# 16x16 diagonal blocks of the triangular inverses by VectorE, two output slots of each RWKV half moved to between gram and inverse, and a cross-attention in which the heads follow one another

## The reference, cut to what matters

```
u = rmsnorm(h);  p = u @ w_in
o_dn = deltanet(p[:, :DN_COLS])      # 8 heads of 128, chunks of 128 tokens: 16 matrices
o_rw = rwkv7(p[:, DN_COLS:])         # 16 heads of 64, in two halves of 8 heads
h = h + concat(o_dn, o_rw) @ w_out
h = h + cross_attention(rmsnorm(h), rmsnorm(mem))    # 4 heads of 128, 256 memory rows
h = h + square(relu(rmsnorm(h) @ w1)) @ w2;  return rmsnorm(h)
```

```
a_strict = where(strict, (k * beta) @ k.T * decay, 0)
lower = a_strict + eye(128);   u, w = solve_triangular(lower, rhs)
```

## Time and profile before

| what | value |
|---|---|
| three runs of the kernel before | 3989.09, 3991.14, 3993.26 us (median 3991.14) |
| the profiled execution | 3994.92 us |
| its span, first to last instruction | 3991.7 us |
| mean granted TensorE clock | 0.955 of full speed |
| TensorE busy | 3712.8 us, 93% of the span |
| VectorE busy | 2413.6 us, 60% |
| ScalarE busy | 1502.7 us, 38% |
| GpSimd busy | 157.9 us, 4% |

### The profile page before, as it was taken

How to read it: one execution, slowest core, us unless ns; L and a number is a source line. 1 busy time by engine, 2 the same in 40 slices (tenths; PEclk the granted TensorE clock), 3 DMA queues, 4 the chain that set the end, 5 groups by cost and what they waited for, 6 DMA issues and landing times.

```text
span 3991.7 us, 54679 instructions
## 1 busy us (share of the span) xinstructions
PE 3712.8 (93%) x22418; PEld 3305.0 (83%) x22418; DVE 2413.6 (60%) x2621; ACT 1502.7 (38%) x1294; POOL 157.9 (4%) x159
## 2 busy tenths in 40 slices
PE   8996899999999999999999999777787969999998
PEld 8985699999988888888888989576676868888887
DVE  3544547977677766666666644456465445566656
ACT  3333333445434333433344433322222343343334
POOL 2000000000000000000000000122121000000000
PEclk8998899999999999999999999798787989999999
DMA  4451444556767765565554544000012425555554
GB/s 178 174 191 51 148 160 174 204 191 221 264 227 244 252 219 200 200 205 200 200 200 155 184 152 156 10 22 32 22 43 106 169 86 189 189 189 189 189 188 148
DMA packets 122889, 650.35 MB, mean 163 GB/s; under 512 B 10737, under 2 KB 43889, under 8 KB 49553
## 3 DMA queue, kind: packets, MB, share of 16 engines
q1 hardware_dynamic: 116224, 620.20, 44.5%
q0 software_dynamic: 6544, 28.44, 1.9%
HBM read 620.81 MB, written 27.79 MB: 162 GB/s over the span
## 4 chain that ended last, share of the span: by engine, by line
PE 87%; DVE 9%; ACT 2%; issue 1%; DMA 1%; DVEq 0%; ACTq 0%; POOL 0%; SPq 0%; PEldq 0%
PE pairs L2312 19%; PE pairs L2313 19%; PE pairs L2314 19%; PE quad L2357 12%; PE quad L2358 6%; DVE w_low L2057 2%; PE quad L2468 1%; PE pairs L2470 1%; PE quad L2398 1%; PE quad L2460 1%; PE quad L2865 1%; ACT w_high L1136 0%; PE quad L2703 0%; DVE arena L1940 0%; PE quad L2788 0%
## 5 line engine op out<-in xcount | busy, mean ns | idle before, releaser
L2057 DVE TENSOR_TENSOR w_low<-ring,w_high 128x2048 fp32r<-128x2048 f32 (+1 forms) x547 | 1253.2, 2292 | 926.8 <-ACT w_high L1136 926.3
L1136 ACT CAST w_high<-ring 128x2048 fp32r<-128x2048 f32 (+1 forms) x547 | 1039.2, 1901 | 1737.4 <-PE pairs L2314 1276.0
L2312 PE MATMUL pairs<-x_t,w_high 128*128 128x256 f32 x2592 | 745.4, 288 | 19.3 <-DVE w_low L2057 10.7
L2313 PE MATMUL pairs<-x_t,w_high 128*128 128x256 f32 x2592 | 738.8, 285 | 0.0
L2314 PE MATMUL pairs<-x_t,w_low 128*128 128x256 f32 x2592 | 738.8, 285 | 0.0
L2357 PE MATMUL quad<-x_t,w_high 128*128 128x512 f32 x1984 | 703.0, 399 | 9.9 <-DVE w_low L2057 9.9
L2312 PE MATMUL pairs<-w_high,act_high 128*128 128x512 f32 x1568 | 613.8, 391 | 10.2 <-DVE w_low L2057 6.5
L2313 PE MATMUL pairs<-w_low,act_high 128*128 128x512 f32 x1568 | 612.9, 391 | 0.0
L2314 PE MATMUL pairs<-w_high,act_low 128*128 128x512 f32 x1568 | 612.4, 391 | 0.0
L2358 PE MATMUL quad<-x_t,w_low 128*128 128x256 f32 x1984 | 558.1, 281 | 0.0
L2312 PEld LDWEIGHTS pairs<-x_t,w_high 128*128 128x128 f32 x2592 | 502.5, 194 | 22.0 <-DVE w_low L2057 11.8
(11 more groups left out here) (526 smaller groups left out, 3487.8 us busy)
## 6 DMA issues: line engine op xcount, KB each, us to landing
ring<-pu SPq DMA_DIRECT2D x128, 1024.0 KB, 4.9
ring<-pv SPq DMA_DIRECT2D x128, 1024.0 KB, 4.9
ring<-f SPq DMA_DIRECT2D x128, 1024.0 KB, 4.7
ring<-win SPq DMA_DIRECT2D x48, 1024.0 KB, 4.9
ring<-dn SPq DMA_DIRECT2D x32, 1024.0 KB, 4.9
ring<-rw SPq DMA_DIRECT2D x24, 1024.0 KB, 4.8
ring<-wout SPq DMA_DIRECT2D x16, 1024.0 KB, 4.9
ring<-wq SPq DMA_DIRECT2D x16, 1024.0 KB, 4.9
```

Of the source, the lines that this page charges most:

```text
L1136: nc.scalar.copy(WH[s % 2][:, 0:w], flat(ring[s])[:, 0:w]).then_inc(ev["split_high"], 1)
L2057: v.tensor_tensor(WL[s % 2][:, 0:w], flat(ring[s])[:, 0:w], WH[s % 2][:, 0:w].bitcast(F32), ALU.subtract).then_inc(ev["split_low"], 1)
L2312: mm(out, stat[0], mov[0], start=start, stop=False, skip_group_check=True)
L2313: mm(out, stat[0], mov[1], start=False, stop=False, skip_group_check=True)
```

## The change

1. **The inverse.** A new function `substitute` on VectorE inverts the 16x16 diagonal blocks of all 16 matrices at once. Transposes of 32x512 lay each block out along the elements of one partition (there are 128 blocks, one a partition); then sizes 2, 4, 8 and 16 are done by elementwise products and sums; then it spreads the results and transposes them back into `Ti` and `Tt`. ScalarE copies two of the four partition groups (`block_cells`), clears `Ti` and `Tt` (RWKV) and makes the masked blocks of the level 16 to 32 (`off16`, four instructions). Of the five levels in the loop two are left (16 to 32, and 32 to 64, whose `Ti` products are 64x64), and then the last. GpSimd masks for one level only. Each of VectorE's 33 instructions in `substitute`, but for a few, waits for the one before.
2. **DeltaNet.** The mask over AM goes (L1760); `a_ready` is told for each group, AM is turned ahead of qd; KD is scaled by ScalarE in eight instructions; the product with beta (L1775) is done in place in VT right behind `substitute`; GpSimd clears `AOFS`, `Ti` and `Tt` early. Three small instructions for two masks (`EVEN16`, `MINUS16`) stand at the beginning of the stage.
3. **RWKV halves.** Output slots 2, 3 and 6, 7 move on TensorE from ahead of `rv_turned` to between gram and inverse, their low parts from VectorE's chain of products to GpSimd behind `decayed`, and `out_add` of them behind `substitute`. `bk_turned` waits for the `out_add` of the two slots before them. The 16 transposes and the four copies to `RAM` go.
4. **Cross-attention.** Maxima, exponentials, scaling (two instructions of one head), transposes, values, high and low part are done for one head after another, with an event for each; the copy to `HID` goes (the high part is read from PSUM); the first slot of wo is made high and low ahead of the last copies of q.

The core of the diff:

```diff
-            for l in range(1, 6):
-                for q in range(4):
-                    if l >= 2:
-
-                        pool.wait_ge(ev["inv_m1"], 4 * l + (24 * c - 5 + q))
-                    between(q, LVA[:, l:l + 1, :])
+            for q in range(4):
+                pool.wait_ge(ev["inv_m1"], 12 * c + 4 + q - 1)
+                between(q, LVA[:, 5:6, :])
...
                 pool.wait_ge(ev["decayed"], hf + 1)
+                nc.gpsimd.memset(flat(AOFS[1 + hf]), 0.0).then_inc(ev["inv_off"], 1)
+                out_low(4 * hf + 2)
+                out_low(4 * hf + 3)
                 pool.wait_ge(ev["gram_out"], 16 * hf + 16)
+                pool.wait_ge(*nth(f"off16_{1 + hf}", 1))
                 inverse_pool(pool, 1 + hf, GR[:, :, 0, :])
...
+        def substitute(dve, o, v, c, A, turned, Ti, Tt):
+
+
+            C, N = COEF[c], INV16[c]
+            o.tell(v.memset(N, 0.0), o.order)
+            for g in range(4):
+                r = slice(32 * g, 32 * g + 32)
+                ins = v.transpose(BLKS[r, :].rearrange("p (c b i) -> p c b i", c=16, b=2),
+                                  A[r, :, 32 * g:32 * g + 32].rearrange("p m (b c) -> p c b m", b=2))
+            o.done(ins)
+            C3 = C[:, 0:256].rearrange("p (c i) -> p c i", c=16)
+            pair = BLKS.rearrange("p (c b i) -> p c b i", c=16, b=2)
+            o.done(v.tensor_scalar(C3, pair[:, :, 0, :], MINUS16[:, 0:1], None, ALU.mult))
+            o.tell(v.memset(N[:, 0:256:17], 1.0), o.order)
+            o.done(v.scalar_tensor_tensor(C3, pair[:, :, 1, :], MINUS16[:, 1:2], C3, ALU.mult, ALU.add))
...
+            for n in (8, 16):
+                h, k = n // 2, 16 // n
...
+                for x in range(k):
+                    ins = v.tensor_tensor(prod[:, x], a21[:, x].unsqueeze(2).broadcast_to([P, h, h, h]),
+                                          n11[:, x].rearrange("p l j -> p j l").unsqueeze(1).broadcast_to([P, h, h, h]), ALU.mult)
+                o.done(ins)
+                o.done(v.tensor_reduce(sums.rearrange("p k i j -> p (k i j)"), prod.rearrange("p k i j l -> p (k i j) l"), AX.X, ALU.add))
...
+            for n, (T_, x) in enumerate(((Ti, N3.rearrange("p i j -> p j i")), (Tt, N3))):
+                o.done(v.tensor_tensor(spread, x.unsqueeze(2).broadcast_to([P, 16, 2, 16]),
+                                       EVEN16.unsqueeze(1).unsqueeze(3).broadcast_to([P, 16, 2, 16]), ALU.mult))
+                if n == 1:
+                    dve.wait_ge(*nth(f"blocks_out{c}", 1))
+                o.tell(v.transpose(BLKS[0:64, :], PRODS[0:64, :]), ev[f"blocks_turned{c}"])
+                for g in (2, 3):
+                    ins = v.transpose(block_cells(T_, g), PRODS[32 * g:32 * g + 32, :].rearrange("p (j b i) -> p j b i", j=16, b=2))
+                o.done(ins, ev["inv_new"])
...
-            with pe.Fori(1, 6, 1) as l:
+            for l in range(2):
...
             o.done(mul(KRS[:, 0], t1(KKN), w(EX[1], 1)), ev["decayed"])
-            out_add(2 * hf + 1)
...
-            dve.wait_ge(ev["gram_out"], 16 * hf + 16)
-            inverse_dve(dve, o, v, 1 + hf, RAM, GR[:, :, 0, :], RTI, RTT, ram)
+            substitute(dve, o, v, 1 + hf, GR[:, :, 0, :], False, RTI, RTT)
+            out_add(2 * hf + 1)
+            inverse_dve(dve, o, v, 1 + hf, RTI, RTT)
...
             pe.wait_ge(ev["gram_out"], 16 * hf + 16)
-            for n in range(4):
-                for i in range(4):
-                    ins = nc.tensor.transpose(PQ[:, n, i * P:(i + 1) * P], GR[:, 4 * n + i, 0, :], ID)
-                ins.then_inc(ev["ram_turned"], 1)
+            for q in (4 * hf + 2, 4 * hf + 3):
+                out_slot(pe, mm, q)
             inverse_pe(pe, mm, 1 + hf, GR[:, :, 0, :], RTI, RTT)
...
+            weights_turned(0)
+            for h in range(1, 4):
+                weights_turned(h)
+                values(h - 1)
+            values(3)
```

More of the change, by code:

```diff
@@ L822, in inverse_act @@
                     act.nop().then_inc(ev["inv_m1_out"], 1)
-            with act.Fori(1, 6, 1) as l:
+            act.wait_ge(ev["inv_off"], OFF0[c] + 1)
+            for g in range(4):
+                r, cols = slice(32 * g, 32 * g + 32), slice(32 * g + 16, 32 * g + 32)
+                ins = nc.scalar.mul(AOFS[c].rearrange("p q m s -> p (q m) s")[r, :, cols], At[r, :, cols], EVEN16[r, 0:1])
+            o.tell(ins, ev[f"off16_{c}"])
+            if c == 0:
+                act.wait_ge(ev["inv_off"], OFF0[c] + 3)
+            else:
+                nc.scalar.copy(Ti, rep(TRI[:, 0:P], 16))
+                o.done(nc.scalar.copy(Tt, rep(TRI[:, 0:P], 16)), ev[f"cleared{c}"])
+            for n, T_ in enumerate((Ti, Tt)):
+                act.wait_ge(*nth(f"blocks_turned{c}", n + 1))
+                for g in range(2):
+                    ins = nc.scalar.copy(block_cells(T_, g), BLKS[32 * g:32 * g + 32, :].rearrange("p (j b m) -> p j b m", j=16, b=2))
+                o.tell(ins, ev[f"blocks_out{c}"])
+            act.wait_ge(*nth(f"blocks_out{c}", 2))
+            act.wait_ge(ev["inv_new"], 14 * c + 2)
+            for l in range(2):
                 for q in range(4):
-                    g = 4 * l + (24 * c - 4 + q)
+                    g = 12 * c + 4 * l + q
                     act.wait_ge(ev["inv_m1"], g + 3)
@@ L920, in stage2_act @@
             for n in range(4):
+                act.wait_ge(*nth("a_turned", n + 1))
+                o.tell(nc.scalar.copy(flat(AT_)[:, BLK * n:BLK * (n + 1)], PP[:, n // 2, n % 2, :]), ev["at_out"])
+            for n in range(4):
                 act.wait_ge(*nth("qd_turned", n + 1))
-                o.tell(nc.scalar.copy(flat(ATN)[:, BLK * n:BLK * (n + 1)], PP[:, n // 2, n % 2, :]), ev["atn_out"])
-            for n in range(4):
-                act.wait_ge(*nth("a_turned", n + 1))
-                o.tell(nc.scalar.copy(flat(AT_)[:, BLK * n:BLK * (n + 1)], PQ[:, n, :]), ev["at_out"])
+                o.tell(nc.scalar.copy(flat(ATN)[:, BLK * n:BLK * (n + 1)], PQ[:, n, :]), ev["atn_out"])
             for n in range(4):
@@ L929, in stage2_act @@
                                       PP[:, n // 2, n % 2, :].rearrange("p (h d) -> p h d", h=4)), ev["v_tok"])
-            inverse_act(act, 0)
+            act.wait_ge(*nth("kd_turned", 1))
+            for h in range(DH):
+                ins = nc.scalar.mul(KD[:, h, :], PQ[:, h // 4, (h % 4) * P:(h % 4 + 1) * P], DST[:, 9, 0, h:h + 1])
+            o.tell(ins, ev["kd_ready"])
+            inverse_act(act, o, 0, AT_, TI, TTI)
             act.wait_ge(ev["qs_mm"], 1)
@@ L2561, in stage2_pe @@
                     ins.then_inc(ev[e], 1)
-            pe.wait_ge(*nth("a_ready", 1))
+            for n in range(4):
+                pe.wait_ge(*nth("a_ready", n + 1))
+                for i in range(4):
+                    ins = nc.tensor.transpose(PP[:, n // 2, n % 2, i * P:(i + 1) * P], AM[:, 4 * n + i, :], ID)
+                ins.then_inc(ev["a_turned"], 1)
             for n in range(4):
@@ L2600, in stage2_pe @@
                 for h in range(DH):
[L2601 removed]
+                    ins = mm(at(0, h), TTI[:, DH * t + h, :], RH[:, h, :] if t else VT[:, 0, h, :], start=True, stop=True)
                 ins.then_inc(ev["vn_mm"], 1)
```

310 lines of the change are left out of this document (188 added, 122 removed).

## The result

The changed kernel takes 3873.23 us (median of 4 runs, 3872.5 to 3874.86), the kernel before 3992.2 beside it: a ratio of 0.9704, with a 95% interval of 0.9687 to 0.9721. The forecast was 3870, in a range of 3843 to 3902; the sum for the profiled execution was 3873.7, and that execution took 3873.07.

A forecast was written before the change was run, and what follows sets the result against it. The inverses were taken as bound by TensorE's product count, on one chain with VectorE's work. Gains 38.8 (DeltaNet), 72.4 (RWKV), 10.6 (cross-attention), less 0.6, made 121.2: 3994.9 to 3873.7 profiled, 3869.9 against the median, forecast 3870, range 3843 to 3902.

The forecast's parts named there:

- S: Time of VectorE's substitution ahead of each inverse, 33 chained instructions, eleven stepped ones at 1.0 us: 19.0 us.
- rivals 3 and 6: 3: stepped operands at the slowest row's price, S 27, 3894 us, chance 0.14; 6: VectorE becomes the bound, slower, 0.03.
- rival 2: Faster still: plain prices for substitution's stepped operands and TensorE's clock held, 3845 us, chance 0.17.
- Rival 5: RWKV halves: moved slots not hidden, first product waits for them; 5 us a half give 3880, chance 0.03.
- The shorter inverse, 27.9: TensorE's remaining levels in each inverse: 14.2 for 16 to 32, 9.4 for 32 to 64, 4.3 for the last.
- The first four at 1.2 GHz, twice 0.89: Inverse's level 16 to 32: four of twelve group instructions at the low clock, the other eight at 0.89 us; 14.2.
- The halves: RWKV: 31.3 us gained per inverse and 4.9 per earlier gram, 72.4 for both; moved slots and low parts cost nothing.
- 4.9 for an earlier gram: Each RWKV half: gram starts 7.9 us earlier, less 3 for TensorE's low clock.
- The 3 us for a gram at the low clock: Each RWKV gram: without slots ahead, a first part runs at 1.2 GHz, costing between nothing and 6; 3 taken.
- Cross-attention: First score to first product with wo, head after head: 15.2 against 25.8 us, gain 10.6, between 3 and 15.
- the way of head 3 alone: End of cross-attention, behind head 3's exponentials: 4.4 us of work and 1.7 for seven hand-overs.
- Rival 4: TensorE stays at 1.2 GHz through the short inverse, 55 us over three, 3925 us, chance 0.08.

The follow-up runs named there:

- turned_plain: Changed kernel with each substitution's four transposes in and four direct transposes out on adjacent elements (wrong blocks inverted): 3864.7 us, ratio 0.967.
- turned_twice: Changed kernel with the first four transposes of each substitution done twice: 3879.36 us, ratio 0.9716.
- warm_both: Changed kernel with 44 unused TensorE identity products ahead of each half's turns, and 40, 10 and 18 ahead of the inverses: 3873.36 us, ratio 0.9696.
- tt_half: Changed kernel with one of two direct transposes and one of ScalarE's two copies left out for `Tt` (wrong inverse): 3870.06 us, one run.
- slots_before: Changed kernel with output slots 2, 3, 6, 7 back ahead of the gram, their low parts back on VectorE: 3875.24 us, ratio 0.9709.
- lows_dve: Changed kernel with only the low parts of slots 2, 3, 6, 7 back on VectorE, slots left between gram and inverse: 3877.05 us, ratio 0.9712.
- warm_gram_long: Changed kernel with 62 and 57 unused TensorE identity products ahead of the two halves' turns of BKS: 3863.79 us, ratio 0.9672.
- lows_early: Changed kernel with GpSimd's two low parts of a half beside VectorE's chain of decayed factors instead of behind it: 3874.72 us, ratio 0.9702.
- control: The changed kernel itself, unedited, timed again beside other runs: 3873.83 us, ratio 0.9697.
- xa_before: Changed kernel with the cross-attention of before, all heads in one step and wo's first slot made ready later: 3889.29 us, ratio 0.974.
- warm_gram: Changed kernel with 44 unused TensorE identity products ahead of the turns of BKS in each half: 3874.67 us, ratio 0.9697.

## Why the prediction was right, step by step

- **S and its prices.** 19.2 us against 19.0; stepped operands 1.01 to 1.07 against the 1.0 that I took between 0.72 and 1.74. turned_plain shows that the step is what costs, and turned_twice that the whole substitution is on the path. That disposes of rivals 3 and 6, and of the half of rival 2 that rests on plain prices. Rival 5 is out too: the slots end 2.8 and 4.4 us ahead of the first group.
- **The shorter inverse, 27.9.** Right as a sum (27.7 in DeltaNet), wrong in its first term. "The first four at 1.2 GHz, twice 0.89" is not what sets the first level: warm_both took that clock away and gained nothing, tt_half took away part of `Tt`'s unpacking and gained. The path goes from `Tt`, 3.6 us behind `Ti` (I had 3.4, and made nothing of it), and not from `Ti`. I had put the start of TensorE at `Ti`'s time and not asked what its second product waits for. The two came out alike since two cold `first` groups last about as long (3.75) as `Tt` is late. The second level was 10.4 and not 9.4: an instruction of full products beside one of 64x64 has a pitch of 1.0, not 0.89.
- **The halves.** The moved slots and GpSimd's low parts were covered as reckoned, but slots_before beside lows_dve shows that the slots' new place bought nothing: the 3.5 us that it frees ahead of the turns are lost again, 3.0 in the gram and 0.4 in the inverse. Of the 4.9 for an earlier gram, 3.9 came in half 0 and 5.5 in half 1. The 3 us for a gram at the low clock were 3.5 and 2.3, and warm_gram_long shows that they were the clock. Half 0's inverse was 2 us longer than forecast. 1.4 of that is the clock, which was at 1.00 when the level began and fell to 0.50 in its middle: lows_early has 44.3 in half 0 without that fall and 45.6 in half 1 with it.
- **Cross-attention.** 13.1 against 10.6. The first exponential came at 2.1, as reckoned. Head 3's exponentials ended at 8.4 instead of 9.1, since ScalarE waited 1.0 and not 1.7. What was most mis-sized is the way of head 3 alone, 4.3 instead of 6.1: its two scalings took 0.62 and not 1.0, its transposes 0.66 and not 0.93, and its seven hand-overs together some 0.3 and not 1.7. I also left out the 1.5 to 2.8 that a clock held up gives to the first products with wo, and didn't say that part of the 25.8 was a wait for wo's first slot.
- **Rival 4** (1.2 GHz through the inverse) is out: from the second product on each inverse ran at the full clock in the changed kernel, but for a few microseconds in half 0.
- **Behind inverse 1.** 3.6 us lost with no edit there, in no term of mine. Over the fourteen profiles the same code took 195.2 to 195.5 us in five, 192.6 in two and 190.6 to 191.8 in seven. The five are the changed kernel, its control, xa_before, warm_gram and warm_both, whose stretches from inverse 0 to inverse 1 agree to 0.15 us; the two are turned_plain and lows_early; the seven are all the others, the kernel before among them. The granted clock over the 20 us of state products that begin 16 us behind the inverse is 0.50 in the five, 0.59 in the two and 0.67 in the seven. This is turned_plain's:

```profile
2904.07:2924.07 20.00, 17.35 (x90) 16.76 (x89) 2.28 (x4) 0.00 (x0) 0.00 (x0) 0.59 0.00 0
```

That the rhythm ahead of it selects the case is what the pattern suggests; no run tested it by itself, and the cause stays open.

That the sum of the gains came out within 1 us is partly luck: 3.6 lost behind inverse 1 and 2 in half 0 stand against 2.5 and 1.5 more from cross-attention, and where the last qd falls moves the span by up to 6 us from run to run by itself.

## What to carry to other kernels

When a level has two products, ask what each operand waits for and put the path at the later one; a cost that lies in the shadow of another (here the low clock of the first groups) is no term of the sum. Work that is moved out of an idle stretch of TensorE can leave a low clock behind: the slots ahead of the gram had kept the gram at the full clock. Products without a use, placed up to the last moment, bought back the 5.9 us of the two grams; the kernel was 10 us faster, 0.25%, but the other 4 can't be planned by anything shown here. Judge a change of 5 us by the cut and not by the total, as stretches without an edit moved by up to 5. And give GpSimd its work where VectorE reads PSUM or one operand of SBUF; beside products of VectorE with both in SBUF one of the two waits, here once VectorE and once GpSimd.

## What the runs showed of the hardware that I had not expected

- With idle gaps of 0.9 us between its work TensorE stayed at 1.2 GHz for all of a 20 us stretch in which it was busy for 17.35 (clock 0.50), and in other runs of the same code had a mean clock of 0.59 or 0.67 in that stretch. The 44 products that ended 4.8 us early gained nothing, 62 that ended 0.75 us early all of it.
- While an instruction of GpSimd of 4.57 us ran, two of VectorE's took 5.59 us instead of 1.29; in another place the same instruction took 9.27 while small ones of VectorE ran at their usual 0.36 to 0.38.
- A transpose of 32 partitions by 512 costs 0.70 us in order and 1.04 stepped, one of 64 partitions in order 0.70 as well.
